# A three-block float32 network on one core: a gate norm's power moved on GpSimd, the first products regrouped, the last norm's roots moved to GpSimd

## The reference, cut to what matters

```python
u = jnp.einsum('bsd,de->bse', x, w_in) + b_in            # first projection of block 1
c = glu_a * jax.nn.sigmoid(glu_b)                        # two of its column groups

def gated_group_rmsnorm(y, z, w):                        # block 3, SSD branch, 4 groups of 256
    g = y.astype(jnp.float32) * jax.nn.silu(z.astype(jnp.float32))
    g = g.reshape(b, l, SSD_GROUPS, NORM_GROUP)
    g = g * lax.rsqrt(jnp.mean(g * g, axis=-1, keepdims=True) + EPS)

_, local = lax.associative_scan(combine, (a, bu), axis=1)  # block 3, S5 branch
states = local + pows * h0[:, None]

gate = jax.nn.sigmoid(rmsnorm(h, ple_norm_w[i]) @ w_ple_gate[i])
h = h + (p[i] @ w_ple_proj[i]) * gate
return rmsnorm(h, final_norm_w)                          # last norm, output
```

## Time and profile before

| what | value |
|---|---|
| median of three runs | 3037.93 us (3037.4 to 3038.45) |
| the profiled execution | 3039.63 us, of which span 3037.8 us |
| PE busy | 2940.9 us, 97% |
| DVE busy | 1638.4 us, 54% |
| ACT busy | 1141.0 us, 38% |
| POOL busy | 1004.6 us, 33% |
| mean granted clock of PE | 0.991 of full speed |

### The profile page before, as it was taken

How to read it: one execution, slowest core, us unless ns; L and a number is a source line. 1 busy time by engine, 2 the same in 40 slices (tenths; PEclk the granted TensorE clock), 3 DMA queues, 4 the chain that set the end, 5 groups by cost and what they waited for, 6 DMA issues and landing times.

```text
span 3037.8 us, 37680 instructions
## 1 busy us (share of the span) xinstructions
PE 2940.9 (97%) x15094; PEld 2378.1 (78%) x15094; DVE 1638.4 (54%) x2686; ACT 1141.0 (38%) x1952; POOL 1004.6 (33%) x725
## 2 busy tenths in 40 slices
PE   8999989999999999999999999999999999999998
PEld 7876668888878888887888866677877778788887
DVE  6989760025545664224233567777656545534436
ACT  3125662222441111223333267546545422332344
POOL 3210002232417786234541212321111234442542
PEclk9999999999999999999999999999999999999999
DMA  4110001113323333113332211342222266543323
GB/s 134 49 42 22 15 15 49 49 56 111 125 78 88 89 90 102 41 55 116 107 124 77 65 31 56 115 124 67 60 65 72 71 175 168 180 141 109 110 78 111
DMA packets 267776, 260.56 MB, mean 86 GB/s; under 512 B 17457, under 2 KB 208049, under 8 KB 266577
## 3 DMA queue, kind: packets, MB, share of 16 engines
q1 hardware_dynamic: 232624, 198.15, 21.9%
q10 hardware_dynamic: 34976, 60.01, 6.2%
HBM read 213.41 MB, written 42.99 MB: 84 GB/s over the span
## 4 chain that ended last, share of the span: by engine, by line
PE 81%; DVE 9%; ACT 5%; DMA 2%; issue 2%; POOL 1%; ACTq 0%; SPq 0%; DVEq 0%
PE psum L581 24%; PE psum L582 24%; PE psum L583 24%; PE psum L587 3%; DVE arena L2971 1%; DMA arena<-in_w_in 1%; PE psum L794 1%; PE psum L764 1%; ACT WS L1240 1%; DVE arena L2428 1%; PE psum L971 1%; PE psum L995 1%; ACT arena L1435 1%; PE psum L1164 1%; DVE XL L2293 1%
## 5 line engine op out<-in xcount | busy, mean ns | idle before, releaser
L3253 POOL TENSOR_TENSOR WS<-arena,WS 128x1024 fp32r<-128x1024 f32 (+1 forms) x295 | 722.7, 2456 | 1644.9 <-ACT WS L1240 1644.8
L581 PE MATMUL psum<-XH,WS 128*128 128x512 f32 x2600 | 1031.3, 397 | 16.0 <-ACT arena L1418 3.4
L582 PE MATMUL psum<-XL,WS 128*128 128x512 f32 x2600 | 1015.5, 391 | 0.0
L583 PE MATMUL psum<-XH,WS 128*128 128x512 f32 x2600 | 1015.3, 391 | 0.0
L581 PEld LDWEIGHTS psum<-XH,WS 128*128 128x128 f32 x2600 | 490.2, 189 | 133.8 <-issue 12.9
L1240 ACT ACTIVATE WS<-arena 128x1024 fp32r<-128x1024 f32 (+1 forms) x295 | 308.2, 1052 | 738.2 <-PE psum L583 247.3
L583 PEld LDWEIGHTS psum<-XH,WS 128*128 128x128 f32 x2600 | 489.7, 188 | 103.6
L582 PEld LDWEIGHTS psum<-XL,WS 128*128 128x128 f32 x2600 | 490.4, 189 | 97.2
L581 PE MATMUL psum<-WS,XH 128*128 128x512 f32 x960 | 377.5, 393 | 9.5 <-POOL WS L3253 7.4
L582 PE MATMUL psum<-WS,XH 128*128 128x512 f32 x960 | 374.3, 390 | 0.0
L583 PE MATMUL psum<-WS,XL 128*128 128x512 f32 x960 | 374.3, 390 | 0.0
(11 more groups left out here) (300 smaller groups left out, 2875.6 us busy)
## 6 DMA issues: line engine op xcount, KB each, us to landing
arena<-in_w_in SPq DMA_DIRECT2D x85, 512.0 KB, 3.8
arena<-in_w_out SPq DMA_DIRECT2D x48, 512.0 KB, 3.7
arena<-in_w_in_even SPq DMA_DIRECT2D x48, 512.0 KB, 4.0
arena<-in_w_out_even SPq DMA_DIRECT2D x32, 512.0 KB, 3.7
h_spill<-arena ACTq DMA_DIRECT2D x24, 512.0 KB, 3.1
arena<-s_table SPq DMA_DIRECT2D x8, 1536.0 KB, 6.9
arena<-in_w_in_odd SPq DMA_DIRECT2D x18, 512.0 KB, 3.8
s_table<-arena SPq DMA_DIRECT2D x32, 256.0 KB, 3.0
```

The costliest lines, as they stand in the source:

```text
L581: e.matmul(ps, wh, xh, start=start, stop=False)
L582: e.matmul(ps, wh, xl, start=False, stop=False)
L583: return e.matmul(ps, wl, xh, start=False, stop=stop)
L3253: e.tensor_tensor(lo, x, hi.bitcast(F32), SUB).then_inc(*w.up("w_lo", u))
```

## The change

Four edits. On POOL, the power of gate norm (3, 1) is issued ahead of `mid(0)` instead of behind it. At the start, POOL clears a 128 x 128 tile `awake`, PE multiplies it with itself 18 times before its first product, and the 24 products of n = 0 and of n = 1 are issued grouped by operand instead of slice by slice: for n = 0 high x high, low weights x high, high x low; for n = 1 high x high, high x low, low weights x high. At the end, the roots of tiles 0 to 6 go from ACT (square root) and DVE (reciprocal) to POOL (power -0.5), seven instructions behind all of its weight splits; DVE forms the means of tiles 0 to 3 ahead of the four final products, and those of tiles 4 to 6 ahead of the next `h4`. Tile 7 keeps ACT's root.

```diff
--- before.py
+++ after.py
@@ -371,6 +371,7 @@
         TURNED = [view(92, S), view(96, S)]
 
         UNITS = [(n, g, hq) for n in range(8) for g in range(2) for hq in range(2)]
+        awake = view(111.5, 128)
         PRU, PTU = [view(84 + 4 * i, 4, 256) for i in range(3)], [view(96 + 4 * i, 2, 512) for i in range(2)]
         STU = [view(104 + i / 16, 12) for i in range(3)]
         BO2, G2 = view(72, 2, 512), view(76, 2, 512)
@@ -680,16 +681,23 @@
                     key = blocks[i][0] + (half,)
                     bank = take(ring, key, *blocks[i][2](half))
                     sl = half_of(half)
-                    if x == "b1" and n == 0 and at is not None:
+                    if x == "b1" and n < 2 and at is not None:
+                        def low():
+                            w.wait_ge("w_lo", u)
+                            for kb in range(8):
+                                t = e.matmul(psum[:, bank, :], hl[1][:, kb, :], XH[:, kb, sl], start=False, stop=n == 1 and kb == 7)
+                            return t
                         w.wait_ge("w_hi", u)
                         for kb in range(8):
                             w.wait_ge("x_hi", x, kb, half)
                             e.matmul(psum[:, bank, :], hl[0][:, kb, :], XH[:, kb, sl], start=kb == 0, stop=False)
+                        if n == 0:
+                            low()
+                        for kb in range(8):
                             w.wait_ge("x", x, kb, half)
-                            e.matmul(psum[:, bank, :], hl[0][:, kb, :], XL[:, kb, sl], start=False, stop=False)
-                        w.wait_ge("w_lo", u)
-                        for kb in range(8):
-                            t = e.matmul(psum[:, bank, :], hl[1][:, kb, :], XH[:, kb, sl], start=False, stop=kb == 7)
+                            t = e.matmul(psum[:, bank, :], hl[0][:, kb, :], XL[:, kb, sl], start=False, stop=n == 0 and kb == 7)
+                        if n == 1:
+                            t = low()
                         t.then_inc(*w.up(*key))
                         continue
                     w.wait_ge("w_lo", u)
@@ -736,6 +744,9 @@
 
             w_in = ap["w_in"]
             ws.pump(2)
+            w.wait_ge("awake")
+            for _ in range(18):
+                e.matmul(psum[:, 7, 0:128], awake, awake, start=True, stop=True)
             proj_first([((f"glu_{ab}", 0, 0), w_in[:, c:c + 128], lambda half, done=done: [(done, 0, half)])
                         for ab, c, done in (("b", 2560, "glu_sig"), ("a", 2048, "glu"))], "b1", None, -1)
             for m in range(1, 4):
@@ -2228,7 +2239,7 @@
             def fin(tile):
                 w.wait_ge("h4", 1, tile)
                 if tile >= 2:
-                    w.wait_ge("nrm_rc", "fin", tile - 2)
+                    w.wait_ge("nrm_ms", "fin", tile - 2)
                 e.activation(SQ3[tile % 2], H3[:, tile, :], ACT.Square, accum_out=small[:, 32 + tile:33 + tile]).then_inc(
                     *w.up("nrm_sq", "fin", tile))
 
@@ -2244,13 +2255,11 @@
             weave((proj_th(), 1, True), (g_evs(4, 4), 1, True))
             for tile in range(4):
                 fin(tile)
-                fin_root(tile)
             weave((proj_tm(512, tiles=range(4, 8)), 1, True), (g_evs(8, 4), 1, True))
             g_ev(12)
             for k in range(3):
                 fin(4 + k)
                 g_ev(13 + k)
-                fin_root(4 + k)
             fin(7)
             fin_root(7)
 
@@ -3220,9 +3229,17 @@
                 w.own()
                 e.tensor_tensor(o, o, sg, A_).then_inc(*w.up("h4", ch, tile))
 
+            def fin_mean(tile):
+                r = small[:, 32 + tile:33 + tile]
+                w.wait_ge("nrm_sq", "fin", tile)
+                e.tensor_scalar(r, r, 1.0 / 1024, 1e-6, M, A_).then_inc(*w.up("nrm_ms", "fin", tile))
+
             def fin(tile, parts=1):
                 r, step = small[:, 32 + tile:33 + tile], 1024 // parts
-                rms("fin", tile, r, 1e-6)
+                if tile < 7:
+                    w.wait_ge("fin_pow", tile)
+                else:
+                    rms("fin", tile, r, 1e-6)
                 w.wait_ge("g3")
                 w.own()
                 for i in range(parts):
@@ -3233,11 +3250,14 @@
             for n in range(8):
                 h4(n)
             for tile in range(4):
+                fin_mean(tile)
+            for tile in range(4):
                 fin(tile)
             for n in range(8, 12):
                 h4(n)
             h4(12)
             for k in range(3):
+                fin_mean(4 + k)
                 h4(13 + k)
                 fin(4 + k)
             fin(7, 2)
@@ -3301,6 +3321,7 @@
                         *w.up("x_lo_p", stage, kb, also=[("x", stage, kb, 0), ("x", stage, kb, 1)]))
 
 
+            e.memset(awake, 0.0).then_inc(*w.up("x_lo_p", "awake", also=[("awake",)]))
             ws.pump(2)
             proj_first(2)
             run(proj_cm(10))
@@ -3472,8 +3493,8 @@
 
             run(proj_cm(1))
             w.wait_ge("ch_y", 3, 7)
+            step("root", 3, 1)
             mid(0)
-            step("root", 3, 1)
             for e_ in range(7):
                 run(proj_cm(2 if e_ else 1))
                 mid(e_ + 1, *([] if e_ < 6 else [lambda: ws.pump(ws.use + 2)]))
@@ -3504,6 +3525,10 @@
             for _ in range(3):
                 run(proj_th())
             run(proj_tm(512, tiles=range(4, 8)))
+            for tile in range(7):
+                r = small[:, 32 + tile:33 + tile]
+                w.wait_ge("nrm_ms", "fin", tile)
+                e.tensor_tensor(r, r, minus_half[:, 0:1], ALU.pow).then_inc(*w.up("x_lo_p", "fin", tile, also=[("fin_pow", tile)]))
 
 
         def sync_program(e, w):
```

## The result

The changed kernel takes 3043.97 us (median of 19 runs, 3038.42 to 3049.19); the kernel before took 3037.66 on the same chip (19 runs, 3036.31 to 3041.28). Its runs also scatter more. The profiled execution took 3047.0 us (span 3045.2), 7.4 more than that of before and 3.0 above the changed kernel's own median, so what is read in it is somewhat more than the median has to explain. A few executions of some kernels took from 3,395 to 11,151 us; the ratios leave them out, and the medians of the tables, which keep them, move by some 0.2 us without them.

A forecast was written before the change was run, and what follows sets the result against it. PE, busy 97%, was taken to bound the kernel with its work and gaps. Middle +0.8, start -1.1 and end +1.4 summed to +1.1 us on the median 3037.93: 3039.0 us, range 3036.0 to 3041.5.

The forecast's parts named there:

- The sum: Whole kernel: middle +0.8, start -1.1 and end +1.4 give +1.1 us, so 3039.0 us.
- the difference is laid on the median: Whole kernel: the +1.1 us forecast on the profiled span is added to the median, 3037.93, giving 3039.0 us.
- The middle: Around the moved power: PE's 7.20 us wait is not gone but stands later; +0.8 us, between -1.7 and +1.7.
- the split: Middle: POOL's weight split, now at 2432.95, makes DVE's L3141 take 2.80 us instead of 0.69.
- the store: Middle: SP's store, which frees the table's place, waits for L3100, ending at 2437.9, 0.4 us later than before.
- the table: Middle: `tab_s` of round 1 lands at 2449.7, so PE waits some 11 us at L1145.
- The clock: Middle: 0 to 1.7 us more of half speed after the idleness ahead of L1145; +0.4 us (0 to 0.9).
- The start: First 48 matmuls: regrouped, they no longer wait early for remainders and end at 23.3; -1.1 us, between -2.2 and +0.2.
- end at 5.7: Start: the 18 extra products take at most 4.7 us, then PE idles until 8.62 and the clock falls.
- rival (c): Start: the extra products keep the clock up, or it rises before 12.8; start -2.2, kernel 3037.9 us; chance 10%.
- The end: Final norm: final products wait for POOL's powers, 4.0 us later, then a shorter chain, 13.7 against 16.3; +1.4 us.
- Rival (d): End: POOL's powers are the bound; at 2.2 us each the end costs +6.5 and the kernel is at 3044; chance 4%.

The follow-up runs named there:

- e1_power: The kernel before with only the power of gate norm (3, 1) moved ahead of `mid(0)`: 3040.32 us, ratio 1.0007.
- e3_final: The kernel before with only the final norm's part: means on DVE, seven powers on POOL; 3039.82 us, ratio 1.0004.
- e4_regroup: The kernel before with only the new order of the first blocks' products, without the 18 awake products: 3038.13 us, ratio 0.9999.
- the first eight experiments: Eight of the twelve follow-up kernels, variants of the kernel before or of the changed kernel; the text does not list which eight.

## Why the prediction was wrong

**The sum** was +1.1. With the sizes measured at the places it spoke of it would have been about +2.4 (+1.4, -0.1, +1.1): that is 3040.3, inside the range. The step that failed is the last one, "the difference is laid on the median": it takes for granted that the rest of the kernel stays as it is, and so puts a term at nothing without a reason. In the profiled execution +7.3 us came up there between 70 and 2389 us, +5.1 of it in half clock; the rest goes with weights that land later. The scatter fits: in the changed kernel's 19 runs the mean clock goes from 0.992 (3038.4 us) to 0.988 (four runs, 3047.2 on the mean), and time and clock go together (correlation -0.79).

**The middle** was sized +0.8 and measured +0.6 to +1.0 in e1_power and +0.6 to +1.4 in the changed kernel, by the ends that one takes. The causes named were right for the split (2.74 us, forecast 2.80), the store (0.4 us later) and the table. Wrong was where PE would stand: I had it at L1164, 1 to 2 us for `h5`, and then 11 us for the table. It stood 4.69 us one step earlier, before L1156, because the accumulating products of round 0 take PSUM bank 6, which the turned rows hold until `y_nrm`. In the profile of before this wait lay hidden under the 7.20 us. The clock I had at +0.4; from 2400 to 2520 us half clock costs 6.8 us before and 6.8 after, so 0. The Trainium skill's rule in "SBUF — State Buffer", "Who interferes with whom", agrees with the 2.74 us; that the small power let L3141 pass in 0.69 it does not explain.

**The start** was sized -1.1 and measured about -0.1. From the first real product to the one behind the 48, the seven traces with the old order took 14.6 to 15.9 us (15.3 on the mean; before 15.5), the five with the new order and the awake products 14.9 to 15.5 (15.2; the changed kernel 15.5), the two with the new order alone 14.7 and 15.8 (15.3). What sets the length is when full clock comes: in the old order 5.5 us after the first product gives 14.6, 7.4 gives 15.5 and 8.3 gives 15.9. At the same rise the new order alone is some 0.2 us shorter. The changed kernel's -0.8 at 70 us is all there when its first real product starts (7.79, forecast 8.62), since its first weights happened to land earlier. The step that failed is the 18 products that "end at 5.7": the eight of L1113, the row they were priced by, are four products, two instructions each, and the 18 end at 7.5. So the clock was up at 8, as rival (c) had it, but (c)'s gain did not come: with the small stalls for ACT it was down again from 12.6 to 15.9.

**The end** was sized +1.4 and measured +1.1 (and +1.1 in e3_final). The first two powers take 0.56 us each (I took 1.0), and only the first stands ahead of a final product; the next two, beside DVE's final products, take 1.24 and 1.42. The last split, put at 3010.1 on before's time, ended 6.3 later, at 3016.38, in a kernel that was 6.2 late. The four final products took 5.45 in place of 5.2, and a tile's step is 3.12 as forecast. The end's table load ends at 3040.87 and ACT's root starts at 3040.88, without a gap of 1.38 us, so the drain that the Trainium skill adds ("ScalarE: Activation LUTs", "What ACT_TABLE_LOAD costs") isn't seen here either. Rival (d), which needed 2.1 us a power, was out.

**Open.** Why the kernel before lies so well. In the traces of before, e1_power, e3_final and e4_regroup the stall at 1,775 us meets the clock's instants in places that differ by 0.4 us only, though the first weights landed up to 0.7 us apart. A start at half clock that ends at one of these instants would tie the two together in part, and the awake products would loosen the tie. The starts above show the first half of it, that the length of the start follows the clock's rise; no run tests the rest. Open too is why some weights land later in the changed kernel. It also stays open how much of the 2.1 us of e1_power is chance: its own trace is faster than that of before.

## What to carry to other kernels

- In a kernel that is all matmul, an edit at the start moves every stall behind it. A stall of some 2 us may or may not cost 1 to 1.7 us at half clock, and a weight may land later for what needs it. So an edit worth 1 or 2 us is not told by its own place: count the half-clock stretches of the whole trace in both kernels, and test with a plain shift.
- A stall that is hidden under a longer one has to be looked for before the longer one is taken away: for each thing PE does in the next 20 us, list every tile, bank and table it takes, and who frees it. Here one name, `y_nrm`, freed two of them, and the power was only the first link to it.
- To be early, all of a chain has to be early: the power alone brought nothing (+0.6 to +1.0 us at its place in the trace), the power with its products and multiplications 7 us.

## What the runs showed of the hardware

- The same stall of 2.32 us, from the same instruction, is followed by full clock in nine traces and by half clock in five, by where the clock's instants fall in it. A stall of 1.92 us can be enough. Over the 167 runs of the changed kernel, the first eight experiments and the kernel before beside them, the time falls by 1.7 us per 0.001 of mean clock within a kernel (correlation -0.68).
- Adding 2.7 us of work to the start of the kernel before costs 8.3 by the medians (7.9 by the ratio); adding 0.9 us to the changed kernel costs nothing that can be measured.
- A float32 power of one column on GpSimd takes 0.54 to 0.56 us, and 1.24 and 1.42 beside DVE's final products; one of four columns takes 1.21 on the mean (1.00 to 1.46).
- A float32 product of 128x128 is two instructions on PE: 18 products were 36, and took 6.5 us at the start, 0.21 us apart at half clock and 0.11 at full.
